# Three of eight slices of a matrix-vector product go from VectorE to TensorE

## The chip, the cores and the metric

The kernel runs on one core of a Trainium2 chip. The metric is the device time of one execution in microseconds (us). A core has the engines TensorE (matmuls, with a weight load, LDWEIGHTS, ahead of each), VectorE, ScalarE, GpSimd and SyncE (SP, which here only issues transfers), each with its own queue of instructions, and 16 DMA engines that they share. In the profile they are PE and PEld, DVE, ACT, POOL and SP.

## The reference

The reference is a network of two blocks on a sequence of 512 tokens with 1024 channels, all in float32: a state-space mixer with a pooling branch, a mixture of 64 experts, a recurrence, and an attention layer. What matters here is how the first block begins:

```
mod = silu(c) @ w_ada[0] + b_ada[0]        # c: (1, 1024), w_ada: (1024, 6 * 1024)
sh1, sc1, g1, sh2, sc2, g2 = split(mod, 6)
u = rmsnorm(h, norm_mix_g) * (1 + sc1) + sh1
proj = u @ w_in                            # all the first mixer is made from it
...
```

The first 2048 columns of `mod` (`sh1`, `sc1`) are needed before `u` and so before any projection. The other 4096 are computed later, beside other work.

## The kernel before

Channels lie on the 128 partitions: `h` and `u` are held as 8 tiles of 128 channels x 512 tokens. Weights stream through six slots of 1 MB (`Weights`, lines 159 to 191): load number i goes to slot i modulo 6, SP waits for whoever used load i - 6 last (`gone`), and issues all loads in one order. `left` notes which engine gives a slot back.

The first 2048 columns of `w_ada` are eight slices of 256 columns, loads 0 to 7 of 1 MB each (`start_sp`, line 326). A slice is a tile of 128 partitions x 8 (k) x 256. Loads 6 and 7 wait for slices 0 and 1 to be used; behind them SP issues `t_dt`, then `t_x`, `t_BC`, `t_z` twice for the first mixer, each when the slot six loads earlier is given back. ScalarE's queue issues the vectors, `h` (`x_t`) in four parts, and the table of constants (`start_act`, line 331).

For each slice s VectorE (`dve_ada`, line 347) multiplies the eight 128x256 parts by silu(c), one scalar to a partition, and adds them up in one of two buffers, `K.ada[s % 2]`. TensorE (`pe_ada`, line 360) then sums over the partitions: two matmuls, with 128 columns of the buffer stationary and a single column of ones moving, into two columns of PSUM bank 6. VectorE may write a buffer again once TensorE has read it (`q.pe.at("ada", s - 2)`).

Beside that, ScalarE squares the tiles of `h` into two buffers (`act_square`, line 303), TensorE adds them up over channels with a matrix of ones (`pe_sum`, line 294, 512 columns moving, 8 times), and ScalarE makes `rstd` from it by Ln and Exp (`act_rstd`, line 311). TensorE's order is in `start_pe` (line 368): slices 0 and 1, all eight sums, slices 2 to 7. VectorE's is in `start_dve` (line 380): slices 0 to 7, then a wait for `rstd` and for the last slice, the sum with `b_ada` into `mod` (line 389), and `u`. Behind `u` TensorE begins with the projection of `decay_pe` (line 448), then the dense products of the first mixer (line 274).

The router, much later, is used below as a comparison: 32 matmuls (line 274) with 128x128 of `u` stationary and 64 columns of `weights` moving, each chain over k adding up in one place of PSUM.

In float32 the profile shows each matmul as two passes, each with its own LDWEIGHTS and MATMUL, so that its counts are twice those of the code.

Of the kernel before, what the change touches and what calls it, by code (L numbers as in the profile page):

```python
# [11 lines left out]
P, T, D, KD, NT = 128, 512, 1024, 8, 4  # L12
# [258 lines left out]
def products(pe, out, terms):  # L271

    for n, (lhsT, rhs) in enumerate(terms):
        last = pe.matmul(out, lhsT, rhs, start=n == 0, stop=n == len(terms) - 1)  # L274
    return last
# [18 lines left out]
def pe_sum(K, q, name, k):  # L294
    pe = K.nc.tensor
    if k == 0:
        K.bank(7, q.act, name, "ln")
    pe.wait_ge(*q.act.at(name, "square", k))
    pe.matmul(K.psum[:, 7, :], K.c("ones"), K.sq[k % 2][:, :], start=k == 0, stop=k == KD - 1) \  # L299
        .then_inc(*q.pe.tick(name, "sum", k))  # L300
# [43 lines left out]
    act_rstd(K, q, "mix")  # L344


def dve_ada(K, q, s, i, after=None):

    dve, acc, w = K.nc.vector, K.ada[s % 2], K.W.tile(i, KD, 256)
    if after is not None:  # L350
        dve.wait_ge(*after)
    dve.wait_ge(*K.W.here(i))
    dve.tensor_scalar(acc[:, :], w[:, 0, :], K.c_act[:, 0:1], None, ALU.mult).then_inc(*q.dve.tick())
    for k in range(1, KD):
        dve.wait_ge(*q.dve.now())
        dve.scalar_tensor_tensor(acc[:, :], w[:, k, :], K.c_act[:, k:k + 1], acc[:, :], ALU.mult, ALU.add) \
            .then_inc(*(q.dve.tick() if k < KD - 1 else K.W.left(i, q.dve)))


def pe_ada(K, q, s, i, col):  # L360
    pe, acc = K.nc.tensor, K.ada[s % 2]
    pe.wait_ge(*q.dve.at("w", i))
    pe.matmul(K.psum[:, 6, col:col + 1], acc[:, 0:P], K.c("ones")[:, 0:1], start=True, stop=True)
    pe.matmul(K.psum[:, 6, col + 1:col + 2], acc[:, P:2 * P], K.c("ones")[:, 0:1], start=True, stop=True) \
        .then_inc(*q.pe.tick("ada", s))


def start_pe(K, A, q, w0):
    pe = K.nc.tensor
    pe.wait_ge(*K.consts_in.at("all_in"))  # L370
    K.bank(6, q.dve, "mod")
    for s in range(2):
        pe_ada(K, q, s, w0 + s, 2 * s)
    for k in range(KD):
        pe_sum(K, q, "mix", k)
    for s in range(2, 8):
        pe_ada(K, q, s, w0 + s, 2 * s)


def start_dve(K, A, q, w0):  # L380
    dve = K.nc.vector
    for n, eps in enumerate((1e-6, 64e-5, 1e-5, 1e-36)):
        dve.memset(K.eps[:, n:n + 1], eps).then_inc(*q.dve.tick(*(("eps",) if n == 3 else ())))
    dve.wait_ge(*q.act.at("c"))
    for s in range(8):
        dve_ada(K, q, s, w0 + s, q.pe.at("ada", s - 2) if s >= 2 else None)
    K.nc.vector.wait_ge(*q.act.at("mix", "rstd"))
    dve.wait_ge(*q.pe.at("ada", 7))
    dve.tensor_tensor(K.mod[:, 0:16], K.psum[:, 6, 0:16], K.col("b_ada", 0, 16), ALU.add) \
        .then_inc(*q.dve.tick("mod"))  # L390
    modulated_dve(K, q, "norm_mix_g", 8)


def modulated_dve(K, q, gain, scale_at):

    dve, g = K.nc.vector, K.stat[:, 0:KD]
    dve.wait_ge(*q.dve.now())
    dve.tensor_scalar(g, K.mod[:, scale_at:scale_at + KD], 1.0, None, ALU.add).then_inc(*q.dve.tick())
    dve.wait_ge(*q.dve.now())
    dve.tensor_tensor(g, g, K.col(gain, 0, KD), ALU.mult).then_inc(*q.dve.tick())  # L400
    for k in range(KD):
        if k == 0:
            dve.wait_ge(*q.dve.now())
        dve.scalar_tensor_tensor(K.u[:, k, :], K.h[:, k, :], g[:, k:k + 1], K.rstd[:, :], ALU.mult, ALU.mult) \
            .then_inc(*q.dve.tick(gain, "scaled", k))
# [515 lines left out]
def combine_pe(K, Y, X, q, before, w0):  # L921
    pe = K.nc.tensor
    K.bank(6, q.dve, "mod")
    for j in range(KD):
        w = w0 + 5 * j
        wg = two_tiles(K, w, KD, P)
        for i in range(2):
            pe.wait_ge(*K.W.here(w))
            K.bank(i, q.act, "gate", j, i)
            products(pe, K.psum[:, i, :], column_terms(wg[:, i], 0, K.u)) \  # L930
                .then_inc(*(q.pe.tick("gate", j) if i == 0 else K.W.left(w, q.pe)))
        if j == 0:
            pe.wait_ge(*before.act.all())
        pe.wait_ge(*K.W.here(w + 1))
        K.bank(2, q.dve, "ssd", j)
        products(pe, K.psum[:, 2, :], column_terms(K.W.tile(w + 1, 16, P), 0, Y, 16)).then_inc(*K.W.left(w + 1, q.pe))
        pe.wait_ge(*K.W.here(w + 2))
        K.bank(3, q.dve, "pool", j)
        products(pe, K.psum[:, 3, :], column_terms(K.W.tile(w + 2, KD, P), 0, X.mixed)).then_inc(*K.W.left(w + 2, q.pe))
        for n in range(2):  # L940
            pe_ada(K, q, 8 + 2 * j + n, w + 3 + n, 2 * (2 * j + n))
# [12 lines left out]
def combine_dve(K, X, q, w0):  # L954
    dve = K.nc.vector
    for j in range(KD):
        w, gate = w0 + 5 * j, X.gate[j % 2]
        for n in range(2):
            dve_ada(K, q, 8 + 2 * j + n, w + 3 + n, q.pe.at("ada", 6 + 2 * j + n) if j else None)
        dve.wait_ge(*q.act.at("gate", j, 1))  # L960
        for i, name in enumerate(("ssd", "pool")):
            dve.wait_ge(*q.pe.at("w", w + 1 + i))
            dve.tensor_tensor(gate[i], gate[i], K.psum[:, 2 + i, :], ALU.mult).then_inc(*q.dve.tick(name, j))
        dve.wait_ge(*q.dve.now())
        dve.tensor_tensor(X.merged[:, j, :], gate[0], gate[1], ALU.add).then_inc(*q.dve.tick("merged", j))
    dve.wait_ge(*q.pe.at("ada", 23))
    dve.tensor_tensor(K.mod[:, 16:48], K.psum[:, 6, 0:32], K.col("b_ada", 16, 32), ALU.add).then_inc(*q.dve.tick("mod"))
# [2513 lines left out]
def first_mixer(K, A):  # L3481
    q0, qd, q1, q2, q3, q4 = (Steps(K, n) for n in "start decay ssd pool comb mixed".split())
    w = K.W.take(8)
    start_sp(K, A, w)
    start_act(K, A, q0)
    start_pe(K, A, q0, w)
    start_dve(K, A, q0, w)
    K.nc.scalar.wait_ge(*q0.dve.at("mod"))
    modulated_act(K, q0, "norm_mix_g", 0)
# [201 lines left out]
```

## Time and profile before

| what | value |
|---|---|
| median of 3 runs | 3088.01 us (3082.47 to 3090.04) |
| the profiled execution | 3083.99 us, its span 3082.7 us |
| mean granted clock of TensorE | 0.951 |
| TensorE busy in the span | 2765.7 us (90%) |
| VectorE busy in the span | 1076.4 us (35%) |
| VectorE reads the sums into `mod` | 45.70 us after the start |
| first projection on TensorE | 48.03 us after the start |

The span goes from the first to the last instruction; the profiled execution's time holds some 1.3 us more. The granted clock is the share of full speed that TensorE was given: 1.00 is 2.4 GHz, 0.50 is 1.2 GHz. All times of rows are us from the start of the span.

### The profile page before, as it was taken

Reading aid. Unit: us, or ns where it says so; the run is one execution under the profiler, and the core shown is the slowest. Engines: PE = TensorE matmul, PEld = TensorE weight load, DVE = VectorE, ACT = ScalarE, POOL = GpSimd, SP = SyncE. Lnnn points to the kernel's source line nnn. Section 1 sums busy time; section 2 is a strip of 40 time slices with the busy share of each in tenths; the row PEclk is TensorE's granted clock in tenths of the full one; section 3 lists DMA queues with packets and bytes.
Section 4 is the critical chain, followed back from the end, with each engine's and each line's share of the span. In section 5 each row is a group of like instructions: output and inputs, shape, how many; then the busy total and the mean of one; then the engine's idle time right before and its main releaser. Section 6 shows DMA issues by size and latency. Waiting matters only on the chain.

```text
span 3082.7 us, 40644 instructions
## 1 busy us (share of the span) xinstructions
PE 2765.7 (90%) x16440; PEld 1663.5 (54%) x16440; DVE 1076.4 (35%) x2331; ACT 718.6 (23%) x1176; POOL 164.6 (5%) x132
## 2 busy tenths in 40 slices
PE   5999997999989799999999479979996988999797
PEld 2666663444437566677676234427875433555443
DVE  7666664322212122222222131016774113333312
ACT  2333331100021111111111020134553212333311
POOL 0000000000000122222222000000000000000000
PEclk8999998999998899999999789989998999999899
DMA  6222111333313598999999513221111211111110
GB/s 238 107 85 82 69 65 44 123 136 123 136 59 138 195 332 286 386 376 374 373 368 362 166 48 121 79 109 41 44 48 48 101 68 36 55 55 55 34 41 27
DMA packets 79045, 434.28 MB, mean 141 GB/s; under 512 B 11888, under 2 KB 12272, under 8 KB 36240
## 3 DMA queue, kind: packets, MB, share of 16 engines
q1 hardware_dynamic: 53296, 366.37, 30.7%
q0 software_dynamic: 15872, 46.16, 6.4%
q10 hardware_dynamic: 9696, 19.18, 1.7%
q8 instruction: 133, 2.18, 0.3%
q14 instruction: 48, 0.39, 0.0%
HBM read 395.95 MB, written 46.20 MB: 143 GB/s over the span
## 4 chain that ended last, share of the span: by engine, by line
PE 78%; DVE 8%; DMA 7%; ACT 5%; issue 2%; SPq 0%; DVEq 0%; POOL 0%; ACTq 0%; POOLq 0%
PE psum_all L274 34%; PE psum_all L1411 10%; PE psum_all L1853 7%; PE psum_all L1458 5%; DMA weights<-t_experts 4%; PE psum_all L3247 4%; PE psum_all L2000 4%; PE psum_all L3120 3%; PE psum_all L284 3%; PE psum_all L299 1%; PE psum_all L629 1%; DVE big L3381 1%; DVE h L3168 1%; DMA h<-x_t 1%; DMA total_rows<-big,rows 1%
## 5 line engine op out<-in xcount | busy, mean ns | idle before, releaser
L274 PE MATMUL psum_all<-u,weights 128*128 128x512 f32 x1024 | 449.8, 596 | 12.2 <-issue 12.2
L274 PE MATMUL psum_all<-big,weights 128*128 128x512 f32 (+1 forms) x768 | 338.1, 595 | 6.7 <-DVE big L3413 4.2
L274 PEld LDWEIGHTS psum_all<-u,weights 128*128 128x128 f32 x1024 | 193.8, 191 | 246.1 <-issue 245.7
L1411 PE MATMUL psum_all<-big 128*128 128x256 f32 (+1 forms) x1280 | 261.5, 383 | 15.4 <-ACT big L1390 15.4
L274 PEld LDWEIGHTS psum_all<-big,weights 128*128 128x128 f32 (+1 forms) x768 | 144.5, 189 | 194.4 <-issue 187.8
L1411 PEld LDWEIGHTS psum_all<-big 128*128 128x128 f32 (+1 forms) x1280 | 210.7, 180 | 53.6 <-ACT big L1390 16.0
L1853 PE MATMUL psum_all<-big,weights 128*128 128x512 f32 x512 | 222.3, 597 | 14.0 <-DVE big L1923 14.0
L1853 PEld LDWEIGHTS psum_all<-big,weights 128*128 128x128 f32 x512 | 98.1, 192 | 138.2 <-issue 134.2
L274 PE MATMUL psum_all<-weights,u 128*128 128x256 f32 (+1 forms) x704 | 153.5, 383 | 9.6 <-ACT u L412 9.6
L274 PEld LDWEIGHTS psum_all<-weights,u 128*128 128x128 f32 x704 | 135.2, 203 | 30.3 <-ACT u L412 10.4
L284 PE MATMUL psum_all<-const_cols,big 128*128 128x128 f32 (+2 forms) x952 | 133.3, 280 | 18.6 <-DVE big L789 11.0
L1411 PE MATMUL psum_all<-weights,big 128*64 128x256 f32 x1024 | 122.5, 400 | 23.7 <-DMA weights<-t_experts 21.2
L284 PEld LDWEIGHTS psum_all<-const_cols,big 128*128 128x128 f32 (+2 forms) x952 | 108.1, 143 | 54.8 <-issue 28.1
L1421 ACT ACTIVATE big<-psum_all 128x256 f32<-128x256 f32 x52 | 20.1, 386 | 503.9 <-PE psum_all L1411 492.9
L1446 DVE COPY big<-psum_all 128x256 f32<-128x256 f32 x52 | 22.1, 424 | 322.9 <-PE psum_all L284 322.9
L1458 PE MATMUL psum_all<-big 128*128 128x512 f32 (+1 forms) x320 | 130.0, 594 | 0.6 <-DVE big L1446 0.6
L3247 PE MATMUL psum_all<-u,weights 128*128 128x512 f32 x256 | 117.0, 602 | 13.9 <-issue 13.9
L274 PEld LDWEIGHTS psum_all<-big 128*128 128x128 f32 (+1 forms) x736 | 88.8, 187 | 70.6 <-ACT big L3327 36.0
L1369 POOL DMA_INDIRECT big<-u_rows,rows x52 | 54.6, 1051 | 1210.6 <-DVE big L1325 1027.3
L3120 PE MATMUL psum_all<-h,weights 128*128 128x512 f32 x256 | 116.0, 598 | 3.2 <-DVE h L3168 3.2
L1411 PEld LDWEIGHTS psum_all<-weights,big 128*64 128x64 f32 x1024 | 87.2, 144 | 53.5 <-issue 26.5
L2000 PE MATMUL psum_all<-weights 64*64 64x64 f32 x3072 | 111.7, 220 | 3.2 <-issue 1.4
(346 smaller groups left out, 3394.8 us busy)
## 6 DMA issues: line engine op xcount, KB each, us to landing
big<-t_experts SPq DMA_DIRECT2D x96, 1024.0 KB, 23.2
weights<-t_experts SPq DMA_DIRECT2D x96, 1024.0 KB, 18.0
weights<-t_ada SPq DMA_DIRECT2D x24, 1024.0 KB, 7.0
weights<-t_rkvg SPq DMA_DIRECT2D x16, 1024.0 KB, 5.5
rwkv_inputs<-big ACTq DMA_DIRECT2D x48, 256.0 KB, 2.0
big<-rwkv_inputs SPq DMA_DIRECT2D x8, 1280.0 KB, 6.8
weights<-t_x SPq DMA_DIRECT2D x8, 1024.0 KB, 4.9
weights<-t_BC SPq DMA_DIRECT2D x8, 1024.0 KB, 4.9
```

What stands on the lines that cost most here:

```text
L274: last = pe.matmul(out, lhsT, rhs, start=n == 0, stop=n == len(terms) - 1)
L284: last = K.nc.tensor.transpose(out, a, K.c("ident")[0:a.shape[0], 0:a.shape[0]])
L299: pe.matmul(K.psum[:, 7, :], K.c("ones"), K.sq[k % 2][:, :], start=k == 0, stop=k == KD - 1) \
L629: ins = pe.matmul(K.psum[:, 6 + i, o + 64 * r:o + 64 * r + 64], X.W[:, r, c, :], X.xdt[:, c, 64 * r:64 * r + 64], start=True, stop=True)
L1369: pool.indirect_dma_start(X.x_rows[b % X.AHEAD], None, K.u_rows, bass.IndirectOffsetOnAxis(ap=K.rows[b % X.TURN][:, 1:2], axis=0), bounds_ ...
L1411: ins = pe.matmul(K.psum[rows, bank, n * F_E:(n + 1) * F_E], xT[:, k, rows], X.part(r, n, KD, F_E)[:, k, :], start=k == 0, stop=k == KD - 1)
L1458: ins = pe.matmul(K.psum[rows, 2 + half, :], X.hidT[b % 2][:, j, rows], X.part(r, 2, 2, D)[:, j, half * 512:half * 512 + 512], start=j == ...
L1853: ins = pe.matmul(K.psum[:, b, :], K.W.tile(w, KD, 256)[:, k, j % 2 * P:(j % 2 + 1) * P], X.mix[c % 2][:, k, :], start=k == 0, stop=k == K ...
L2000: ins = pe.matmul(K.psum[half(r), b, HEAD * i:HEAD * (i + 1)], lhsT[half(r), i, :], rhs[half(r), i, :], start=True, stop=True)
L3120: ins = pe.matmul(K.psum[:, j % 2, :], K.W.tile(w, KD, 256)[:, k, j % 2 * P:(j % 2 + 1) * P], K.h[:, k, :], start=k == 0, stop=k == KD - 1)
L3168: dve.scalar_tensor_tensor(K.h[:, k, :], X.out[:, k, :], K.col(gain, at + k), K.h[:, k, :], ALU.mult, ALU.add) \
L3247: ins = pe.matmul(K.psum[:, b, :], w[:, i, :], src[:, i, :], start=i == 0, stop=i == KD - 1)
```

## The change

TensorE computes slices 1, 3 and 5 by itself. The new `pe_ada_whole` takes the eight 128x128 parts of each half of a slice as stationary and the matching column of silu(c) as the one moving column, and adds them up in PSUM: 16 matmuls for a slice, where `pe_ada` has two. TensorE gives back the slots of these slices. VectorE keeps slices 0, 2, 4, 6 and 7, with the two buffers taken in turn: 0, 4 and 7 in the first, 2 and 6 in the second; slice 4 waits for TensorE's use of 0, 6 for that of 2, 7 for that of 4. TensorE's order is new: the sums of squares go in pairs between the slices.

```diff
+def ada_sums(K, s):
+    return K.ada[(s // 2 if s < 7 else 0) % 2 if s < 8 else s % 2]
 def dve_ada(K, q, s, i, after=None):
-    dve, acc, w = K.nc.vector, K.ada[s % 2], K.W.tile(i, KD, 256)
+    dve, acc, w = K.nc.vector, ada_sums(K, s), K.W.tile(i, KD, 256)
...
+def pe_ada_whole(K, q, s, i, col):
+    pe, w = K.nc.tensor, K.W.tile(i, KD, 256)
+    pe.wait_ge(*K.W.here(i))
+    pe.wait_ge(*q.act.at("c"))
+    for half in range(2):
+        ins = products(pe, K.psum[:, 6, col + half:col + half + 1],
+                       [(w[:, k, half * P:half * P + P], K.c_act[:, k:k + 1]) for k in range(KD)])
+    ins.then_inc(*K.W.left(i, q.pe))
 def start_pe(K, A, q, w0):
...
-    for s in range(2):
-        pe_ada(K, q, s, w0 + s, 2 * s)
-    for k in range(KD):
+    pe_ada(K, q, 0, w0, 0)
+    pe_ada_whole(K, q, 1, w0 + 1, 2)
+    for k in (0, 1):
         pe_sum(K, q, "mix", k)
-    for s in range(2, 8):
+    pe_ada_whole(K, q, 3, w0 + 3, 6)
+    for k in (2, 3):
+        pe_sum(K, q, "mix", k)
+    pe_ada(K, q, 2, w0 + 2, 4)
+    pe_ada_whole(K, q, 5, w0 + 5, 10)
+    for k in (4, 5):
+        pe_sum(K, q, "mix", k)
+    pe_ada(K, q, 4, w0 + 4, 8)
+    for k in (6, 7):
+        pe_sum(K, q, "mix", k)
+    for s in (6, 7):
         pe_ada(K, q, s, w0 + s, 2 * s)
 def start_dve(K, A, q, w0):
...
-    for s in range(8):
-        dve_ada(K, q, s, w0 + s, q.pe.at("ada", s - 2) if s >= 2 else None)
+    for s, before in ((0, None), (2, None), (4, 0), (6, 2), (7, 4)):
+        dve_ada(K, q, s, w0 + s, q.pe.at("ada", before) if before is not None else None)
```

## Rows read from the trace of the kernel before

**Rows 1.** The page: TensorE's busy time, and the chain that ended last by engine

```profile
PE 2765.7 (90%) x16440; PEld 1663.5 (54%) x16440; DVE 1076.4 (35%) x2331; ACT 718.6 (23%) x1176; POOL 164.6 (5%) x132
...
PE 78%; DVE 8%; DMA 7%; ACT 5%; issue 2%; SPq 0%; DVEq 0%; POOL 0%; ACTq 0%; POOLq 0%
```

**Rows 2.** That chain in order of time, 0 to 60 us: start, length, what

```profile
3.41 22.33 DMA h<-x_t
...
26.44 1.98 PE psum_all L299 x4
...
44.04 0.50 DVE ada_sums L356
...
45.70 0.19 DVE mod L389
...
48.03 8.42 PE psum_all L448 x16
```

**Rows 3.** Timeline of VectorE, 5 to 46 us: start, length, what [idle before]

```profile
6.92 0.35 DVE L353 TENSOR_SCALAR ada_sums<-weights,c_act 128x256 f32<-128x256 f32 x1 [5.94 <-DMA weights<-t_ada]
7.30 3.61 DVE L356 SCALAR_TENSOR_TENSOR ada_sums<-weights,c_act,ada_sums 128x256 f32<-128x256 f32 x7
...
28.80 0.35 DVE L353 TENSOR_SCALAR ada_sums<-weights,c_act 128x256 f32<-128x256 f32 x1 [5.37 <-PE psum_all L364]
```

**Rows 4.** DMA issues: of 10.5 to 11.5 us (slice 6), of 14 to 16 us (slice 7)

```profile
weights<-t_ada SPq DMA_DIRECT2D x1, 1024.0 KB, 17.7
...
weights<-t_ada SPq DMA_DIRECT2D x1, 1024.0 KB, 16.3
```

**Rows 5.** Timeline of TensorE's matmuls, 14 to 29 us

```profile
14.48 0.58 PE L363 MATMUL psum_all<-const_cols,ada_sums 128*128 128x1 f32 x2 [14.48 <-DMA const_cols<-shape_consts]
14.93 0.56 PE L364 MATMUL psum_all<-const_cols,ada_sums 128*128 128x1 f32 x2
15.36 0.57 PE L363 MATMUL psum_all<-const_cols,ada_sums 128*128 128x1 f32 x2
...
16.21 5.67 PE L299 MATMUL psum_all<-sq,const_cols 128*128 128x512 f32 x8
...
28.41 0.36 PE L364 MATMUL psum_all<-const_cols,ada_sums 128*128 128x1 f32 x2
28.63 0.36 PE L363 MATMUL psum_all<-const_cols,ada_sums 128*128 128x1 f32 x2
```

**Rows 6.** Timeline of TensorE's weight loads in the sums of squares

```profile
17.20 0.34 PEld L299 LDWEIGHTS psum_all<-sq,const_cols 128*128 128x128 f32 x1 [0.52 <-issue]
18.06 0.34 PEld L299 LDWEIGHTS psum_all<-sq,const_cols 128*128 128x128 f32 x1 [0.52 <-issue]
...
23.21 0.19 PEld L299 LDWEIGHTS psum_all<-sq,const_cols 128*128 128x128 f32 x1 [0.24 <-ACT sq L308]
23.64 0.19 PEld L299 LDWEIGHTS psum_all<-sq,const_cols 128*128 128x128 f32 x1 [0.24 <-issue]
```

**Rows 7.** The router: timeline of TensorE, then stretches: PE busy, granted clock, DMA

```profile
922.81 13.92 PE L274 MATMUL psum_all<-weights,u 128*128 128x64 f32 x64 [9.59 <-ACT u L412]
936.51 4.54 PE L284 MATMUL psum_all<-const_cols,u 128*128 128x128 f32 x32
...
922.80:936.50 13.70, 13.69 (x64) 0.50 0.01 2
...
938.00:940.00 2.00, 2.00 (x19) 0.92 0.06 23
```

**Rows 8.** Stretches of 2 us at the start: PE busy, granted clock, DMA share, GB/s

```profile
32.00:34.00 2.00, 0.61 (x4) 0.95 0.72 238
...
50.00:52.00 2.00, 2.00 (x4) 0.79 0.00 0
```

**Rows 9.** Timeline of ScalarE, 28 to 31 us: Ln and Exp for `rstd`

```profile
28.47 0.69 ACT L319 ACTIVATE rstd<-psum_all,stat 128x512 f32<-128x512 f32 x1
...
30.46 0.63 ACT L321 ACTIVATE rstd<-rstd 128x512 f32<-128x512 f32 x1
```

More of the change, by code:

```diff
@@ L360, in pe_ada @@
 def pe_ada(K, q, s, i, col):
-    pe, acc = K.nc.tensor, K.ada[s % 2]
+    pe, acc = K.nc.tensor, ada_sums(K, s)
     pe.wait_ge(*q.dve.at("w", i))
```

## The prediction

> **What bounds the kernel now.** I read the page first [rows 1]: TensorE is busy 90% of the span and carries 78% of the chain that ended last. But the change touches only the first 46 us, so the next view is that chain in order of time [rows 2]. There TensorE hardly appears before 48 us. The chain is the load of `h` (until 25.7 us), the sums of squares on TensorE (26.4 to 28.4 us), then VectorE's slices one after another until 44.5 us, TensorE's two products of the last slice, VectorE's read of `mod` at 45.70 us, and after 2.3 us of `u` TensorE's first projection at 48.03 us. From there TensorE is nearly dense, and all the weights that it needs next have landed. So what this change is worth is the shift of the moment 45.70 us, plus what TensorE's clock does in the projection behind it.
>
> VectorE's own rows [rows 3] show why that moment is so late. A slice is one product of 0.35 us and seven of 3.61 us together, 3.91 us from start to start of the next. Eight slices are 31.3 us, begun at 6.92 us when the first slice lands; the rest of the way to 44.5 us is waiting, above all 5.37 us before 28.80 us, for TensorE, whose small products for slice 2 are queued behind all eight sums of squares.
>
> **What the change removes.** Three slices leave VectorE: 3 x 3.91 = 11.7 us. The wait of 5.37 us can go too, since TensorE's products are now interleaved with the sums. If VectorE alone counted, slices 6 and 7 would follow the landing of slice 6 (issued at 10.9 us, when slice 0 is done, and 17.7 us under way: 28.6 us [rows 4]) and end at 36.4 us.
>
> **What it adds: the price of a whole slice on TensorE.** `pe_ada_whole` has 2 halves x 8 = 16 products, each with a 128x128 stationary of its own and one moving column. The trace of before has the same form in `pe_ada` [rows 5]: each product is two passes; the starts at 14.93 and 15.36 us are 0.43 us apart, those at 28.41 and 28.63 us 0.22 us apart. This is the weight load, at the half clock (1.2 GHz) and at the full one (2.4 GHz); nothing wide is streamed under which it could lie. So a whole slice is 16 x 0.427 = 6.8 us at the half clock and 16 x 0.217 = 3.5 us at the full one, against 3.91 us on VectorE. The sums of squares: loads 0.86 us apart at 17.20 and 18.06 us, 0.43 us apart at 23.21 and 23.64 us [rows 6]. A sum is two such passes, 1.71 us or 0.86 us. `pe_ada` is 0.85 or 0.43 us. From below, the price of a one-column product is bounded by the 0.22 us of the full clock; from above by the 0.58 us that such a product takes from start to end when it stands alone [rows 5]. I take the spacing at the clock that is granted, because the router's 64 passes (its 32 products with 64 moving columns accumulate over k just as these do) take 13.92 us, 0.217 us each at the half clock [rows 7].
>
> **Which clock.** TensorE begins at 14.48 us, when the constants land, at the half clock (the granted column reads 1.00 there, but the spacings are those of the half clock). In the kernel before it goes over to the full clock inside the run of sums that starts at 16.21 us. In the new order 14.48 us is followed by 0.85 us of `pe_ada` and a whole slice. Does a dense run of one-column products raise the clock? The router is the nearest row: TensorE is busy without a gap from 922.8 us on, mostly loading weights, and the granted clock stays at 0.50 through all 13.9 us; it rises some 2 us into the wider 128-column stream that follows [rows 7]. One column is less to stream than 64, so I take it that the whole slices don't raise it. The Trainium skill bears on this in TensorE: Matmul & The Clock Gate, section "What's actually happening": the throttled clock is the default and activity releases it. Read as "any dense work", it would give the rival "full clock early" below; the router's rows speak against that reading.
>
> The other wide streams are the sums, now in pairs: 2 x 1.71 = 3.4 us at the half clock between two whole slices. In the projection from 48.03 us the clock rose after some 2.8 us of wide streaming (0.79 granted in the slice from 50 to 52 us, [rows 8]), at the start only after more than the 1.85 us to 18.06 us and before 23.21 us [rows 6]. So a pair may or may not raise the clock, and a whole slice at the full clock may let it fall again: it fell at 33.8 us in before, when since 28.3 us there had been nothing but one-column products [rows 8]. The last four sums, with only `pe_ada` of slice 4 between, are 6.8 us of nearly wide work and will raise it.
>
> **The sum, no rise before the last sums.** TensorE, in its order:
> - 14.48 + 0.85 (slice 0) + 6.83 (slice 1) = 22.2 us
> - + 3.42 (sums 0, 1) + 6.83 (slice 3) = 32.4 us
> - + 3.42 (sums 2, 3) + 0.85 (slice 2) = 36.7 us
> - + 6.83 (slice 5) = 43.5 us
> - + 3.42 (sums 4, 5) = 46.9 us, where the clock rises; + 0.43 (slice 4) = 47.4 us; + 1.71 (sums 6, 7) = 49.1 us.
>
> ScalarE's squares and the loads of `h` are long there. `rstd` needs from the last sum 0.05 us and then 28.47 to 31.09 us of the trace (Ln, table load, Exp) [rows 9] = 2.7 us: 51.8 us. VectorE: slice 6 shares a buffer with slice 2 and waits for its `pe_ada`, 36.8 to 40.7 us; slice 7 waits for that of slice 4, 47.5 us, and ends at 51.4 us. Its `pe_ada` and VectorE's start at `mod` took 1.16 us at the half clock, about 0.7 at the full one: 52.1 us, 52.5 if the clock rises later. So `mod` moves from 45.70 to 52.1 us: +6.4 us (to +6.8). The end of the chain is then TensorE with its weight loads, no longer VectorE.
>
> Behind `mod`, the projection of 16 passes starts 2.3 us later as before. It ran 2.8 us at the half clock in before; from the rises seen (some 2 us after the router, over 1.85 and under 7 us at the start) I take 3.4 us, costing half the difference, +0.3 us, with -0.5 and +2.1 as bounds (1.85 and 7 us). What follows moves rigidly.
>
> **What costs nothing.** The load of slice 7 now waits for TensorE's slice 1 (22.3 us) in place of VectorE's (14.9 us). SP's queue behind it holds `t_dt` and the first `t_x`, `t_BC`, `t_z`. But slice 6, issued at 10.9 us, lands only at 28.6 us and slice 7, issued at 14.9 us, at 31.2 us, because the queue is full; issued at 22.3 us it is still in time to land there, and its user starts at 47.5 us. Uncovered, it would cost VectorE nothing before 31 us. `t_x` goes out at 32.4 us and `t_z` at 43.6 us, when slices 3 and 5 are done, and the dense products that use them follow the projection, which ended at 56.4 us in before [rows 2] and ends later now: there are over 10 us of cover.
>
> Total +6.4 + 0.3 = +6.7 us. The profiled execution took 3083.99 us (span 3082.7 and 1.3 around it) and would take 3090.7 us; the median of the runs, 3088.01 us, stands 4.0 us above it, so I predict 3094.7 us.
>
> **Rivals.**
> - **A pair of sums raises the clock.** For it: the projection's 2.8 us. If the first pair does by 25.6 us and each whole slice runs at 3.4 us, then 29.0, 30.7 (sums), 31.2, 34.6 (slice 5), 36.3, 36.7 us; slice 7 on VectorE 36.8 to 40.7, `mod` 41.3 us: -4.4 us. If the clock falls during or after every whole slice, as at 33.8 us, most of that is given back: 5 us more, `mod` near 46 us, +0.3 us, and some +0.3 in the projection. I put this rival at -4.4 to +0.6 us, more often near its upper end: 3084 to 3088.6 us, middle 3088 us.
> - **Full clock early.** Against it the router. If it rose at some 20 us: slice 1 done by 21.2, sums 22.9, slice 3 26.4, sums 28.1, slice 2 28.6, slice 5 32.0, sums 33.8, slice 4 34.2, sums 35.9, `rstd` 38.6 us; VectorE ends slice 7 at 38.2 and `mod` is at 38.9 us: -6.8 us, 3081.2 us. By that sentence of the Trainium skill, read widely, it would be this.
> - **Slower than the noise: the products don't follow each other at the spacing of the loads.** If each of the 48 costs what one alone takes, 0.58 us, that is 48 x 0.15 = +7.3 us on top: +14 us, 3102 us. For it: here each product accumulates on the one before in a single column. Against: the router. It decides from 0.05 us a product, where +6.7 becomes +9.3.
>
> **How the numbers follow.** A measurement of this kernel can tell about 0.3% (9.3 us) from no change. Chances: no rise before the last sums 0.50, a pair raises it 0.36, full clock early 0.06, products slower 0.08. The first has its own range of +5 to +9 us, 3093 to 3097.5, and up to 2 us more on either side from the clock elsewhere in the kernel (the runs shown spread 7.6 us). The range goes from the middle of the second rival less that spread, 3083, to 3098 us. Slower by over 0.3%: the fourth and a fifth of the first, 0.17; faster: a small part of the second and third, 0.03; else 0.80.
>
> **What would show it.** LDWEIGHTS of `pe_ada_whole` 0.21 us apart per pass; granted clock 0.50 through slices 1 and 3; VectorE's slice 7 waiting for TensorE's products of slice 4; `mod` at 52 us. Wrong if the clock rises on the first pair (`mod` at 41 to 46 us), or if a pass takes over 0.25 us.

## The result, and the profile after

The changed kernel takes 3095.6 us (median of 11 runs, 3089.07 to 3098.56); the kernel before, over 11 runs, 3084.93 us (3081.48 to 3090.04). The ratio is 1.003, 95% interval 1.002 to 1.0039: slower, by 6 to 12 us, at the edge of the 0.3% that a measurement tells from no change. The forecast was 3094.7 us. The number is near for two reasons that cancel: the median of three runs from which the forecast started (3088.01 us) stands 3.1 us above that of eleven, and the sum of +6.7 us lacks 4.0 us against the 10.7 us between the medians, most of them lost at another place. That the number comes so near is luck.

The profiled execution of the changed kernel took 3093.86 us, its span is 3092.5 us, 9.8 us over that of before. First the start. Timeline of TensorE's matmuls, changed kernel, columns as in [rows 5] (`pe_ada` is now L368 and L369, the whole slices are L274, the projection is L475):

```profile
14.66 0.59 PE L368 MATMUL psum_all<-const_cols,ada_sums 128*128 128x1 f32 x2 [14.66 <-DMA const_cols<-shape_consts]
15.11 0.56 PE L369 MATMUL psum_all<-const_cols,ada_sums 128*128 128x1 f32 x2
15.53 6.96 PE L274 MATMUL psum_all<-c_act,weights 128*128 128x1 f32 x32
22.36 3.76 PE L299 MATMUL psum_all<-sq,const_cols 128*128 128x512 f32 x4
25.91 6.83 PE L274 MATMUL psum_all<-c_act,weights 128*128 128x1 f32 x32
...
36.87 6.96 PE L274 MATMUL psum_all<-c_act,weights 128*128 128x1 f32 x32
43.69 3.76 PE L299 MATMUL psum_all<-sq,const_cols 128*128 128x512 f32 x4
47.24 0.42 PE L368 MATMUL psum_all<-const_cols,ada_sums 128*128 128x1 f32 x2
47.53 0.36 PE L369 MATMUL psum_all<-const_cols,ada_sums 128*128 128x1 f32 x2
47.76 1.96 PE L299 MATMUL psum_all<-sq,const_cols 128*128 128x512 f32 x4
...
55.03 8.38 PE L475 MATMUL psum_all<-u,weights 128*32 128x512 f32 x16 [2.44 <-ACT u L439]
```

TensorE has no idle time from 14.66 to 50 us. Slice 1 takes 6.83 us from its start to the start of what follows (15.53 to 22.36), slice 5 6.82 us: 32 passes of 0.213 us, the half clock. The first three pairs of sums take 3.55 us each, the half clock too, and slice 3, right behind such a pair, 6.69 us: pair and slice together 10.24 us. Sums 6 and 7 are done in 1.8 us, and the two products of slice 4 take 0.29 us and then 0.23 us. So the clock rose right behind the last sum of the third pair, between 47.2 and 47.8 us.

VectorE's timeline, changed kernel, answers to [rows 3]:

```profile
37.04 0.35 DVE L358 TENSOR_SCALAR ada_sums<-weights,c_act 128x256 f32<-128x256 f32 x1 [10.36 <-PE psum_all L369]
...
47.93 0.35 DVE L358 TENSOR_SCALAR ada_sums<-weights,c_act 128x256 f32<-128x256 f32 x1 [6.89 <-PE psum_all L369]
48.32 3.61 DVE L361 SCALAR_TENSOR_TENSOR ada_sums<-weights,c_act,ada_sums 128x256 f32<-128x256 f32 x7
52.70 0.17 DVE L416 TENSOR_TENSOR mod<-psum_all,vector_cols 128x16 f32<-128x16 f32 x1 [0.77 <-PE psum_all L369]
```

VectorE has its 11.7 us of work less, and waits 17.3 us for TensorE's products of slices 2 and 4, where in before it waited 5.37 us for those of slice 2. `mod` is read at 52.70 us, 7.0 us after the 45.70 us of before. SP's queue did no harm: slice 7 was issued at 22.3 us and took 8.6 us, as this row of the DMA issues (22 to 23.5 us) has it, so it was there at 31 us as in before [rows 4]:

```profile
weights<-t_ada SPq DMA_DIRECT2D x1, 1024.0 KB, 8.6
```

From the projection at 55.03 us on, every TensorE pass of the changed kernel comes 6.9 to 7.0 us after the one of before, up to some 1000 us. The other 2.9 us of the span are the net of shifts both ways, with each pass compared with the same one of before: 3.3 us less between 1000 and 2080 us, 3.9 us more from 2080 to 2350 us, 2.3 us more behind that. The first belongs to the profile of before: all the other eight profiles take 2.3 to 3.1 us less than it in that stretch too. The 3.9 us are in the recurrence stage, where TensorE runs thousands of 64x64 products. Here its timeline from 2088 us on, before and changed kernel:

```profile
2087.81 5.77 PE L2000 MATMUL psum_all<-weights 64*64 64x64 f32 x190
2093.51 1.09 PE L284 MATMUL psum_all<-const_cols,big 128*128 128x128 f32 x8
```

```profile
2090.39 6.29 PE L2027 MATMUL psum_all<-weights 64*64 64x64 f32 x208
2098.28 0.68 PE L2027 MATMUL psum_all<-weights 64*64 64x64 f32 x16 [1.60 <-issue]
2098.89 1.09 PE L284 MATMUL psum_all<-const_cols,big 128*128 128x128 f32 x8
...
2279.58 0.92 PE L2027 MATMUL psum_all<-const_cols,weights 64*64 64x64 f32 x25
2282.45 0.45 PE L2027 MATMUL psum_all<-const_cols,weights 64*64 64x64 f32 x7 [1.96 <-issue]
```

In the middle of a run of products of one form TensorE stands still for 1.60 us, and 186 us later for 1.96 us, and the profile names no releaser ("issue"). In before the same products follow each other without a gap; its one stop of this kind over 0.3 us in this stage is 0.94 us long and ends at 2294.02 us. The prediction did not have these waits; the experiments had to tell whether they are chance or belong to the change.

### The profile page after: what moved, and what is told of

Same layout as the page of the kernel before. It is cut to its first block and busy times, and to the rows that moved or that the text cites. A ratio compares the mean times of both kernels' runs of the same rounds, so it can differ in the third digit from the quotient of the medians.

```text
span 3092.5 us, 40788 instructions
## 1 busy us (share of the span) xinstructions
PE 2787.8 (90%) x16524; PEld 1682.5 (54%) x16524; DVE 1065.4 (34%) x2307; ACT 718.4 (23%) x1176; POOL 164.8 (5%) x132
## 3 DMA queue, kind: packets, MB, share of 16 engines
q8 instruction: 133, 2.18, 0.3%
## 5 line engine op out<-in xcount | busy, mean ns | idle before, releaser
L274 PE MATMUL psum_all<-u,weights 128*128 128x512 f32 x1024 | 451.0, 597 | 12.2 <-issue 12.2
L274 PE MATMUL psum_all<-big,weights 128*128 128x512 f32 (+1 forms) x768 | 338.5, 596 | 6.7 <-DVE big L3440 4.2
L274 PEld LDWEIGHTS psum_all<-u,weights 128*128 128x128 f32 x1024 | 194.2, 192 | 247.0 <-issue 246.6
L274 PEld LDWEIGHTS psum_all<-big,weights 128*128 128x128 f32 (+1 forms) x768 | 144.7, 189 | 194.7 <-issue 188.1
L274 PE MATMUL psum_all<-weights,u 128*128 128x256 f32 (+1 forms) x704 | 153.5, 383 | 9.6 <-ACT u L439 9.6
L274 PEld LDWEIGHTS psum_all<-weights,u 128*128 128x128 f32 x704 | 135.3, 203 | 30.3 <-ACT u L439 10.4
L284 PE MATMUL psum_all<-const_cols,big 128*128 128x128 f32 (+2 forms) x952 | 133.3, 280 | 18.5 <-DVE big L816 11.0
L284 PEld LDWEIGHTS psum_all<-const_cols,big 128*128 128x128 f32 (+2 forms) x952 | 108.0, 143 | 54.8 <-issue 28.1
L274 PEld LDWEIGHTS psum_all<-big 128*128 128x128 f32 (+1 forms) x736 | 88.6, 187 | 70.7 <-ACT big L3354 36.1
L274 PE MATMUL psum_all<-big 128*128 128x4 f32 (+2 forms) x736 | 92.8, 254 | 23.8 <-ACT big L3354 15.8
```

The source lines that it names most:

```text
L284: last = K.nc.tensor.transpose(out, a, K.c("ident")[0:a.shape[0], 0:a.shape[0]])
```

## The experiments

Two questions: is it the half clock, and the one moving column behind it, that makes the change slow; and where does the rest of the 10.7 us between the medians come from. Medians of before in these comparisons are 3085.9 us (24 runs, first four kernels) and 3086.07 us (29 runs, last four).

**128 moving columns.** The edit in `pe_ada_whole`; the 128 sums of a half are equal, later slices write over the ones not wanted:

```diff
-        ins = products(pe, K.psum[:, 6, col + half:col + half + 1],
-                       [(w[:, k, half * P:half * P + P], K.c_act[:, k:k + 1]) for k in range(KD)])
+        ins = products(pe, K.psum[:, 6, col + half:col + half + 128],
+                       [(w[:, k, half * P:half * P + P], K.c_act[:, k:k + 1].to_broadcast([P, 128])) for k in range(KD)])
```

> The changed kernel, but each product of a whole slice streams 128 columns (the same column of silu(c) 128 times) in place of one; only the first of the 128 sums is used. Theory (narrow products leave TensorE at its half clock, and that is what makes the change slow): the 128 columns fit under the weight load, so a pass stays at 0.21 us at the half clock, the clock rises some 2 to 4 us after 14.6 us, and stays; passes are then 0.11 us apart, slices 3 and 5 take 3.5 us each, mod is read at 39 us (38 to 41) in place of 52.7, and the time is 7 us under before (3 to 9 under), 14 to 17 us under the change. Rival (the number of weight loads sets the time whatever the clock does, or the clock waits for something else): mod at 52 us or later, time as the change or, if the 128 columns come on top of the load, 48 x 0.2 = 10 us more.

Timeline of TensorE, this kernel:

```profile
15.21 6.69 PE L274 MATMUL psum_all<-c_act,weights 128*128 128x128 f32 x32
21.73 1.88 PE L299 MATMUL psum_all<-sq,const_cols 128*128 128x512 f32 x4
23.45 3.73 PE L274 MATMUL psum_all<-c_act,weights 128*128 128x128 f32 x32
...
29.10 3.82 PE L274 MATMUL psum_all<-c_act,weights 128*128 128x128 f32 x32
...
39.07 0.38 PE L368 MATMUL psum_all<-const_cols,ada_sums 128*128 128x1 f32 x2 [1.93 <-DVE ada_sums L361]
```

```profile
39.78 0.17 DVE L416 TENSOR_TENSOR mod<-psum_all,vector_cols 128x16 f32<-128x16 f32 x1 [0.77 <-PE psum_all L369]
```

The 128 columns cost nothing: at the half clock a pass still takes 0.21 us. The clock rose at the end of the first slice (the sums behind it take 1.7 us a pair), and slices 3 and 5 take 3.6 and 3.7 us. `mod` is read at 39.78 us: 12.9 us before the changed kernel, with the same count of loads, matmuls and waits. The mechanism is as forecast. The time is not: 3084.73 us, ratio 0.9996 (0.9987 to 1.0005), where 7 us under before was expected and the start has gained 5.8 us. About 5 us are lost behind the start here too.

**64 moving columns**, the same edit with 64, one run.

> As the run with 128 columns, but with 64, as the router has. Theory (the router's case, half the load's time is streaming): the clock stays at the half level through slices 1, 3 and 5 at least, each 6.8 us; mod at 50 to 53 us, time as the change. Rival (any dense stream of more than one column raises it): as the run with 128 columns, mod near 39 us.

```profile
15.20 7.07 PE L274 MATMUL psum_all<-c_act,weights 128*128 128x64 f32 x32
22.06 3.32 PE L299 MATMUL psum_all<-sq,const_cols 128*128 128x512 f32 x4
25.21 3.68 PE L274 MATMUL psum_all<-c_act,weights 128*128 128x64 f32 x32
```

Slice 1 runs at the half clock to its end, 6.86 us, as the router's rows had it. But then the first pair of sums raised the clock (3.15 us in place of 3.55, and slice 3 is fast), and it did not fall again: `mod` at 41.55 us. So the expectation for slices 3 and 5 failed: in this run the first slice of 64 columns did not raise the clock, and the next two kept it. Time 3084.79 us, a single run, too few to compare.

**TensorE's order alone.** The kernel before, all slices on VectorE:

```diff
-    for k in range(KD):
+    for k in range(4):
         pe_sum(K, q, "mix", k)
-    for s in range(2, 8):
+    pe_ada(K, q, 2, w0 + 2, 4)
+    for k in (4, 5):
+        pe_sum(K, q, "mix", k)
+    pe_ada(K, q, 3, w0 + 3, 6)
+    for k in (6, 7):
+        pe_sum(K, q, "mix", k)
+    for s in range(4, 8):
         pe_ada(K, q, s, w0 + s, 2 * s)
```

> The kernel before with all eight slices on VectorE; only TensorE's order is changed: sums 0 to 3, the products of slice 2, sums 4 and 5, those of slice 3, sums 6 and 7, the rest. Theory (the wait of 5.37 us on VectorE came from the order alone, and can be had without giving TensorE any slice): VectorE's slices follow each other from 15.5 us, mod at 40.2 us, 5.5 us under before, so the time 5 to 6 us under before if nothing later changes it. Rival (slice 4 has to wait for something else, the landing at 22.7 us or the sums): mod at 43 us or more.

```profile
40.33 0.17 DVE L395 TENSOR_TENSOR mod<-psum_all,vector_cols 128x16 f32<-128x16 f32 x1 [1.18 <-PE psum_all L364]
```

VectorE's slices follow each other from 15.61 us without a wait, `mod` is read at 40.33 us, 5.4 us under before. The time is 3079.42 us, ratio 0.9981 (0.9971 to 0.999), 3 to 9 us under before. By the medians it is 6.5 us under before. The wait of 5.37 us that the change also set out to remove goes without giving TensorE any slice. And here nothing is lost later.

**A delay alone.** The kernel before, VectorE computes slice 7 three times (`dve_again` does the work of `dve_ada` and gives nothing back):

```diff
     for s in range(8):
+        if s == 7:
+            for _ in range(2):
+                dve_again(K, q, s, w0 + s, q.pe.at("ada", s - 2))
         dve_ada(K, q, s, w0 + s, q.pe.at("ada", s - 2) if s >= 2 else None)
```

> The kernel before, with VectorE computing slice 7 three times, so that mod is read 7.8 us later (53.5 us) and nothing else changes. It tests the 10.7 us between the medians, of which the trace has 7.0 before the first projection. Theory A (a delay at the start is passed on rigidly, the rest of the 10.7 us is chance in where the clock falls and rises later, in both kernels): time 7.8 us over before, interval about 6 to 10. Theory B (a delay of this size moves later stages against the clock or against each other, and costs some 3 to 4 us more in every run): 11 to 12 us over before. Theory C (the rest comes from something that the change alone has, its later loads or its 84 more TensorE passes): 7.8 us here, and the change's extra is not seen.

`mod` is read at 53.97 us (+8.3), and in this execution the clock rose late in the projection, which adds 1.3 us. The time is 3094.24 us, 8.3 us over before; ratio 1.0028 (1.0017 to 1.0038), 5 to 12 us. The interval alone doesn't part theory A from B. The traces do: from 2080 to 2350 us this kernel and the one with the new order take 1.2 and 0.9 us less than before; the changed kernel takes 3.9 us more, the one with 128 columns 4.5 us, with 64 columns 2.8 us. What the last three share is not the moment but `pe_ada_whole`: 84 passes more, each with its load, and three waits, 171 instructions more on TensorE before anything else of the program.

The page of the profile of before has a row for instructions: queue q8, 133 packets, 2.18 MB, that is 16 KB each. The trace of before has 34,049 TensorE instructions, 256 to a packet. In the changed kernel one of these packets falls just into the first gap; DMA queues from 2095.5 to 2098.5 us:

```profile
q1 hardware_dynamic: 190, 0.57, 48.4%
q8 instruction: 1, 0.02, 1.8%
```

So the theory was: 171 instructions more at the start shift the borders of the blocks against the program, and in the stage where TensorE uses instructions fastest it reaches some borders before the block is there.

**172 instructions that do nothing.** The kernel before, with 43 useless one-column products where TensorE waits anyway; the trace counts 172 instructions more than in before, for the 171 of the change:

```diff
+def idle_products(K, n):
+    for _ in range(n):
+        K.nc.tensor.matmul(K.psum[:, 5, 0:1], K.vec[:, 0:P], K.vec[:, 0:1], start=True, stop=True)
 def start_pe(K, A, q, w0):
     pe = K.nc.tensor
+    pe.wait_ge(*K.vec_in.at("all_in"))
+    idle_products(K, 24)
     pe.wait_ge(*K.consts_in.at("all_in"))
...
     for s in range(2, 8):
         pe_ada(K, q, s, w0 + s, 2 * s)
+        idle_products(K, {3: 5, 4: 5, 5: 5, 6: 4}.get(s, 0))
```

> The kernel before with 43 useless one-column products more on TensorE, 24 while it waits for the constants and 19 in its waits for VectorE's slices 4 to 7, none on the path: 172 instructions, as many as the change adds (171). mod stays at 45.7 us. Theory (the added instructions shift TensorE's 16 KB blocks of instructions, 256 to a block, against the program, so that in the recurrence stage TensorE waits for blocks where it did not; with the change and with the wide products this stage took 4 to 6 us more than in the kernel before, in the two other runs none): the time is 3 to 5 us over before, and TensorE shows idle times of about 2 us with no releaser near 2085 and 2275 us. Rival (those waits come from the moment at which the stage begins against the clock, not from the count): same as before within 1 us. The useless products write a column of PSUM that nobody reads.

`mod` is read at 45.39 us: no cost at the start. Timeline of TensorE in the recurrence stage, this kernel:

```profile
2083.60 6.29 PE L2009 MATMUL psum_all<-weights 64*64 64x64 f32 x207
2091.77 1.04 PE L2009 MATMUL psum_all<-weights 64*64 64x64 f32 x17 [1.89 <-issue]
...
2275.49 0.92 PE L2009 MATMUL psum_all<-const_cols,weights 64*64 64x64 f32 x25
2278.10 0.45 PE L2009 MATMUL psum_all<-const_cols,weights 64*64 64x64 f32 x7 [1.69 <-issue]
```

The two gaps are there, at the same products as in the changed kernel: with 17 (there 16) passes left of the first run, and between the 25th and the 7 last of the second. The stage takes 5.8 us more than in before. The gaps themselves are 3.6 us of that; behind each the granted clock is at 0.50 for a while, and the eight passes of L284 behind the first, which take 1.09 us in before, take 1.97 us here. In the changed kernel this is so behind the second gap:

```profile
2284.00:2286.00 2.00, 2.00 (x31) 0.50 0.00 0
```

The time is 3088.67 us, ratio 1.0011 (1.0002 to 1.002), 1 to 6 us over before for instructions that cost nothing where they stand; the median (+2.6 us) is a little under the expected 3 to 5, the profiled run (3090.18 us) is within it.

**128 columns and a whole block.** The kernel with 128 columns and `idle_products(K, 21)` ahead of the wait for the constants. The expectation counts a wait with them and comes to 256; the traces have 34,304 TensorE instructions in this kernel and 34,049 in before, 171 + 84 = 255 more, one short of a block.

> The run with 128 columns, with 21 useless one-column products more while TensorE waits for the constants: 84 instructions and a wait, so that the shift against the kernel before is 256, a whole block. mod as there, at 39.8 us. Theory (blocks): the 4 to 6 us lost in the recurrence stage come back; time 5 to 7 us under before (median near 3080), against 1 us under before without them. Rival (moment, not count): as without them, 0 to 2 us under before.

3079.34 us, ratio 0.998 (0.9971 to 0.9989): 3 to 9 us under before. By the medians, each against before in its own rounds, that is 6.7 us under, where the same kernel without the 21 products was 1.2 us under. `mod` is read at 39.14 us, 0.6 us earlier, and the projection gives that back. From 2080 to 2350 us it takes 0.2 us more than before. Timeline from 2083 us:

```profile
2082.80 3.84 PE L2035 MATMUL psum_all<-weights 64*64 64x64 f32 x124
2086.58 1.09 PE L284 MATMUL psum_all<-const_cols,big 128*128 128x128 f32 x8
```

The gap is gone. Adding 21 useless matmuls made the kernel faster, by some 5.6 us.

**The change and a whole block.** The changed kernel with the same 21 products.

> The changed kernel with the same 21 useless products: shift 256. mod at 52 to 53 us where no pair of sums raises the clock, 45 to 47 where one does. Theory (blocks): 3.5 us less than the change, so 4 to 7 us over before in place of 10.7. Rival: 10 us over before as the change.

3090.33 us, ratio 1.0014 (1.0005 to 1.0023), 1.5 to 7 us over before, 4.3 us by the medians, where the change was 10.7 us over. The recurrence stage takes 0.5 us more than before, 3.4 us less than in the changed kernel. Not all of the rest is the blocks: in this profile `mod` is read 3.1 us and the projection ends 2.7 us earlier than in the profile of the changed kernel. In its profile the rival "a pair of sums raises the clock" came true. TensorE's timeline, and stretches of 2 us with the granted clock in the fourth place, this kernel:

```profile
25.28 3.94 PE L274 MATMUL psum_all<-c_act,weights 128*128 128x1 f32 x32
29.07 3.76 PE L299 MATMUL psum_all<-sq,const_cols 128*128 128x512 f32 x4
...
33.34 6.96 PE L274 MATMUL psum_all<-c_act,weights 128*128 128x1 f32 x32
```

```profile
26.00:28.00 2.00, 2.00 (x21) 1.00 0.99 410
28.00:30.00 2.00, 2.00 (x10) 0.61 1.00 415
30.00:32.00 2.00, 2.00 (x4) 0.50 0.95 305
```

The clock rose in the first pair, slice 3 took 3.8 us, and while these one-column products ran the clock fell again, at 28.4 us; slice 5 was slow. `mod` is read at 49.62 us, not at the expected 45 to 47. With 64 and 128 columns the clock stayed up at this place.

```profile
49.62 0.17 DVE L424 TENSOR_TENSOR mod<-psum_all,vector_cols 128x16 f32<-128x16 f32 x1 [1.02 <-ACT rstd L321]
```

**Where the stops stand.** The traces can be counted: how many of TensorE's instructions (loads, matmuls, waits) come before a stop. Between 2040 and 2360 us the ten traces have 33 stops of over 0.25 us with no releaser. The count before every one of them leaves 189, 190 or 191 when divided by 256. The first gap stands behind 16,830 instructions in the changed kernel and with 128 and 64 columns, behind 16,829 with the 172 that do nothing; the second behind 26,045 and 26,046. So these stops are at block borders.

The six stops of over 1.5 us (two in the changed kernel, two with the 172 instructions, one each with 128 and 64 columns) also have the packet in common: TensorE goes on 2.2 to 2.4 us after the last packet of instructions began. And that packet began late. At the first gap of the changed kernel TensorE passed the border before at 2092.7 us and was at the next 4.0 us later, but the next packet began only at 2096.04 us, 3.3 us after that border. From 2089.5 to 2096.0 us q8 has no row at all, and a load has the DMA engines:

```profile
q1 hardware_dynamic: 116, 1.19, 52.0%
big<-rwkv_inputs SPq DMA_DIRECT2D x1, 1280.0 KB, 6.6
```

In the other three kernels with this gap the packet began 3.3 to 3.7 us after the border, in before and with the whole block it began 1.6 to 2.3 us after the border that fell near this load. At the second gap it was 6.0 us in both kernels that have it.

**A version put together from this:** 128 columns, the 21 products, and this order on TensorE:

```diff
     pe_ada(K, q, 0, w0, 0)
     pe_ada_whole(K, q, 1, w0 + 1, 2)
-    for k in (0, 1):
-        pe_sum(K, q, "mix", k)
-    pe_ada_whole(K, q, 3, w0 + 3, 6)
-    for k in (2, 3):
+    for k in range(4):
         pe_sum(K, q, "mix", k)
     pe_ada(K, q, 2, w0 + 2, 4)
-    pe_ada_whole(K, q, 5, w0 + 5, 10)
     for k in (4, 5):
         pe_sum(K, q, "mix", k)
-    pe_ada(K, q, 4, w0 + 4, 8)
+    pe_ada_whole(K, q, 3, w0 + 3, 6)
     for k in (6, 7):
         pe_sum(K, q, "mix", k)
+    pe_ada(K, q, 4, w0 + 4, 8)
+    pe_ada_whole(K, q, 5, w0 + 5, 10)
```

> A version put together from what the runs showed: whole slices on TensorE with 128 moving columns, sums of squares before slices 3 and 5 and the products of slice 4 ahead of slice 5, and the 21 useless products for the block. Expected: clock full from about 20 us, VectorE's slice 6 from 28.7, slice 7 from 33 us, mod at 37.5 to 38.5 us (7 to 8 us under before); the time 7 to 8 us under before, near 3078. Rival (rstd or slice 5 ends last, or the clock falls in between): mod at 40 us or later, time 5 us under before or less.

VectorE's timeline, this kernel:

```profile
28.64 0.35 DVE L358 TENSOR_SCALAR ada_sums<-weights,c_act 128x256 f32<-128x256 f32 x1 [1.93 <-DMA weights<-t_ada]
33.05 0.35 DVE L358 TENSOR_SCALAR ada_sums<-weights,c_act 128x256 f32<-128x256 f32 x1 [0.41 <-PE psum_all L369]
37.82 0.17 DVE L422 TENSOR_TENSOR mod<-psum_all,vector_cols 128x16 f32<-128x16 f32 x1 [0.77 <-PE psum_all L369]
```

`mod` at 37.82 us, 7.9 us under before, as expected; slice 6 now waits for its landing, the bound that the prediction had for VectorE alone. The time is 3076.47 us (7 runs), ratio 0.9971 (0.9959 to 0.9982), 6 to 13 us under before and 9.6 by the medians, more than the 7 to 8 expected: it beats both kernels.

## Why the prediction was right, and where it was not

- **The price of a whole slice** was right: 0.213 us a pass at the half clock, 6.83 us a slice, measured 6.83, 6.69 and 6.82. The rival of 0.58 us a product fell: accumulating in one column costs nothing extra.
- **The clock** was right for the changed kernel's profile: half through slices 1, 3 and 5, full from the end of the third pair on. That this is the cause, and not the number of loads, the run with 128 columns shows: same instructions, `mod` 12.9 us earlier. The rival of a pair that raises the clock is real, though it did not hold in the changed kernel's own profile: it came in two other profiles with its order. With 64 columns, where the clock stayed up, `mod` came at 41.55 us (priced 41.3); in the change with 21 more products, where it fell again, at 49.62 us, 3.9 us after before, and the prediction had priced that at +0.3. How often each case comes in the changed kernel stays open; its runs spread over 9.5 us.
- **The reading of "activity".** The rule of the Trainium skill that was weighed (TensorE: Matmul & The Clock Gate, "What's actually happening") says that activity releases the throttle. Read as any dense work it does not fit this trace: TensorE had no gap from 14.66 to 43.69 us, 20.3 us of it whole slices, and stayed at the half clock all the while. With 128 columns in the same slices the clock was up by 21.73 us.
- **The sum at the start.** `mod` was to come at 52.1 us (to 52.5), and came at 52.70. Of the 0.6 us, 0.2 is the later landing of the constants (14.66 in place of 14.48 us). A pair of sums takes 3.55 us in place of 3.42, but the narrow products behind it take 0.13 us less, so that slice 5 ends at 43.69 us, still only 0.2 us late. The third pair and the products of slice 4 add 0.2 us, because the clock rose behind the pair and not with its end (4.07 us in place of 3.85), and the last slice on VectorE and the products behind it add the rest. In the projection the clock rose after some 2.8 us, as in before, not after 3.4, so the +0.3 us for it was not there (8.4 us in both). Start of the projection: +7.0 us, sum +6.7.
- **"What follows moves rigidly" failed.** It held up to 1000 us. In the recurrence stage the 171 added instructions cost TensorE waits for blocks of instructions: +2.6 us by the median of the run that adds 172 to before, 5.6 us by the pair with 128 columns with and without the 21 products, 3.4 us of the stage by the profiles of the change with and without them. Counting instructions was no part of the working, and the row that would have led there, q8 with its 133 packets, was on the page.
- **The base.** The median of three runs was 3.1 us too high against that of eleven. Sum and base missed by about as much, with opposite signs. The eleven are a little low themselves: in the later rounds before had 3085.9 and 3086.07 us, so that some 1 us of the missing 4.0 may be scatter.
- **What costs nothing** was right: the later loads of slice 7, `t_x` and `t_z` delayed nobody.

What stays open: what makes the packets late. At the first gap the load of `rwkv_inputs` has the DMA engines while the packet is due (0.88 of their time from 2092.7 to 2096.0 us), at the second another load of it for most of the time (0.73 from 2274 to 2280 us); neither load was moved or left out. Lateness alone is not enough: in before one packet begins 3.9 us after its border (2167.9 us), and TensorE, which takes 6.4 us for that block, does not stop. The remaining drift between single profiles, up to 4 us around 2350 to 2410 us, goes with where the clock falls and rises, and no run here takes it apart.

## What to carry to other kernels

A matmul with one moving column cost its weight load here (0.213 us a pass), and a stream of them left TensorE at its half clock; 128 columns in place of one cost nothing and raised it. When work goes to an idle engine, add up that engine's chain at the clock that it will really have: 3 x 6.8 us replaced 3 x 3.9 us. And look first whether the order alone gives the gain: it gave 5.4 us at `mod` here with no work moved. When two kernels differ in the number of TensorE's instructions, look for stops without a releaser, and compare them also with the count filled up towards a whole block, as the 21 useless products did here (171 to 255).

## What the runs showed of the hardware that was not expected

- Instructions that cost nothing where they stand can cost 3 to 5 us elsewhere. TensorE's are fetched in packets of 16 KB, 256 instructions each. With 171 or 172 instructions more at the start there were waits of 1.6 to 2.2 us in the 64x64 products; with 255 more the longest was 0.75 us. A wait lasts until 2.2 to 2.4 us after the packet began, and the packets concerned began 3.3 to 6.0 us after the border before. The Trainium skill (Runtime: NRT & Kernel Launch, "Instruction fetch mechanics") has the blocks of 256 instructions and says that crossing one is mostly hidden. Over the whole kernel that agrees; in this stage it doesn't, by 1.60 and 1.96 us at two borders of the changed kernel.
- The clock, once raised, fell at 28.4 us while one-column products ran without a gap, and stayed full where the same products had 64 columns, though the 6.86 us of the first slice with 64 columns had not raised it. Both are single profiles.
